# Two transformer blocks on one core: SBUF addresses of the matmul operands moved, so that moving data and weights lie at other distances modulo 256 bytes

## The reference

```python
# first block (modulated by w_ada)
proj = h @ w_in                     # q, k, v, g_ret, u, gate_r, gate_s
y_ret = (silu(g_ret) * ret) @ w_ret_out
glu_a, glu_b = split(y_ssm @ w_s5_glu)
merged = sigmoid(gate_r) * y_ret + sigmoid(gate_s) * (glu_a * sigmoid(glu_b))
x = x + gt_m * rmsnorm(merged @ w_out)
x = x + gt_f * rmsnorm((silu(a) * b) @ w_ffn_out)      # a, b = split(h @ w_ffn_in)
# second block
proj = h @ w_in                     # attention, GLA, convolution and merge columns
mixed = g0 * (o_att @ w_br_attn) + g1 * (o_gla @ w_br_gla) + g2 * (y_conv @ w_br_conv)
x = x + mixed @ w_out
x = x + (silu(h2 @ w_gate) * (h2 @ w_up)) @ w_down
return rms_norm(x)
```

## Time and profile before

| | |
|---|---|
| median of 3 runs | 3368.33 us (3368.28 to 3370.02) |
| the profiled execution, its own time | 3367.02 us |
| its span | 3365.2 us |
| granted TensorE clock, mean over the span | 0.992 |
| PE busy | 3294.1 us (98%) |
| DVE busy | 2325.3 us (69%) |
| ACT busy | 1454.6 us (43%) |

### The profile page before, as it was taken

How to read it: one execution, slowest core, us unless ns; L and a number is a source line. 1 busy time by engine, 2 the same in 40 slices (tenths; PEclk the granted TensorE clock), 3 DMA queues, 4 the chain that set the end, 5 groups by cost and what they waited for, 6 DMA issues and landing times.

```text
span 3365.2 us, 51972 instructions
## 1 busy us (share of the span) xinstructions
PE 3294.1 (98%) x20368; PEld 2916.3 (87%) x20368; DVE 2325.3 (69%) x2503; ACT 1454.6 (43%) x1464; POOL 434.4 (13%) x309
## 2 busy tenths in 40 slices
PE   7999999999999999999899999999999999999998
PEld 3599999999888888888778888888888888888887
DVE  6789979877676666666666567657777766666554
ACT  2256664444444444433454444344344444444332
POOL 1047678500100000000000000000003000000000
PEclk9999999999999999999999999999999999999999
DMA  9884556677545555577534444555555555555554
GB/s 381 347 330 182 181 195 238 242 299 299 225 159 191 189 193 193 184 274 260 214 126 175 163 163 178 196 183 188 193 188 198 188 191 195 187 189 193 187 193 150
DMA packets 119746, 706.34 MB, mean 210 GB/s; under 512 B 13776, under 2 KB 28752, under 8 KB 41312
## 3 DMA queue, kind: packets, MB, share of 16 engines
q1 hardware_dynamic: 109280, 695.96, 56.4%
q10 hardware_dynamic: 10368, 9.02, 0.8%
HBM read 702.83 MB, written 2.10 MB: 209 GB/s over the span
## 4 chain that ended last, share of the span: by engine, by line
PE 86%; DVE 7%; ACT 3%; issue 2%; DMA 1%; SPq 1%; DVEq 0%; ACTq 0%
PE acc L643 44%; PE acc L644 22%; PE acc L640 5%; PE acc L641 5%; PE acc L642 5%; DVE ring_lo L1482 2%; DVE ring_raw L1504 1%; ACT ring_hi L1022 1%; DMA ring_raw<-w_ada 1%; SPq L547 1%; PE p_norm L692 1%; PE p_y L710 1%; PE p_z L720 1%; DVE mg L1497 0%; DVE rstd L1529 0%
## 5 line engine op out<-in xcount | busy, mean ns | idle before, releaser
L1482 DVE TENSOR_TENSOR ring_lo<-ring_raw,ring_hi 128x2048 fp32r<-128x2048 f32 (+2 forms) x560 | 1266.9, 2264 | 560.1 <-ACT ring_hi L1022 559.3
L643 PE MATMUL acc<-h_split,ring_hi 128*128 128x512 f32 x4736 | 1644.0, 392 | 9.7 <-DVE h_split L1544 4.5
L644 PE MATMUL acc<-h_split,ring_lo 128*128 128x256 f32 x4736 | 1318.3, 278 | 0.0
L1022 ACT ACTIVATE ring_hi<-ring_raw 128x2048 fp32r<-128x2048 f32 (+2 forms) x560 | 1042.6, 1866 | 451.0 <-DMA ring_raw<-w_down 148.5
L643 PEld LDWEIGHTS acc<-h_split,ring_hi 128*128 128x128 f32 x4736 | 892.4, 188 | 203.7 <-issue 10.5
L644 PEld LDWEIGHTS acc<-h_split,ring_lo 128*128 128x128 f32 x4736 | 890.6, 188 | 0.4
L643 PE MATMUL acc<-ffn_split,ring_hi 128*128 128x512 f32 x1408 | 483.8, 389 | 0.0
L2151 POOL TENSOR_TENSOR sq_sum<-sq_sum,tile 128x256 f32<-128x256 f32 x60 | 77.0, 1284 | 2548.9 <-ACT tile L1048 2548.9
L644 PE MATMUL acc<-ffn_split,ring_lo 128*128 128x256 f32 x1408 | 390.9, 278 | 0.0
L640 PE MATMUL acc<-h_split,ring_hi 128*128 128x256 f32 x1152 | 330.4, 287 | 0.3 <-ACT val_a L1035 0.2
L641 PE MATMUL acc<-h_split,ring_hi 128*128 128x256 f32 x1152 | 322.3, 280 | 0.0
(11 more groups left out here) (381 smaller groups left out, 3936.4 us busy)
## 6 DMA issues: line engine op xcount, KB each, us to landing
ring_raw<-w_ff SPq DMA_DIRECT2D x88, 1024.0 KB, 4.8
ring_raw<-w_down SPq DMA_DIRECT2D x64, 1024.0 KB, 4.8
ring_raw<-w_ffb SPq DMA_DIRECT2D x56, 1024.0 KB, 4.8
ring_raw<-w_mix SPq DMA_DIRECT2D x48, 1024.0 KB, 4.8
ring_raw<-w_ada SPq DMA_DIRECT2D x32, 1024.0 KB, 11.8
ring_raw<-w_heads SPq DMA_DIRECT2D x32, 1024.0 KB, 4.8
ring_raw<-w_ret SPq DMA_DIRECT2D x32, 1024.0 KB, 4.9
ring_raw<-w_glu SPq DMA_DIRECT2D x32, 1024.0 KB, 4.8
```

What stands on the lines that cost most here:

```text
L643: mm(dst[:], hi[s][:, t, :], moving[:, k, :], start=start, stop=False, skip_group_check=True)
L644: return mm(dst[:, T:], lo[s][:, t, :], moving[:, k, 0:T], start=False, stop=stop, skip_group_check=True)
L1022: run(hi[s][:, 0:n, :], raw[s][:, 0:n, :], COPY).then_inc(hi_done, 1)
L1482: tt(lo[s][:, 0:n, :], raw[s][:, 0:n, :], hi[s][:, 0:n, :], SUB).then_inc(lo_done, 1)
```

## The change

It moves operands in SBUF, by other spacers and by reading two of them at an offset. `normed` and `h_split` get 128 bytes more; the first block's mixer stages use the view 128 bytes further (`normed_mix`, `h_mix`), all later stages the one at the start (`h`). The ring's slots get spacers, so that the slots lie alike modulo 256. No instruction is added or taken away on PE, ACT, POOL or SP, and their order is the same; DVE has two more register instructions.

```diff
-LO_AT = slice(16, 16 + KT * P)
...
-                raw.append(sb(shared, f"ring_raw{s}", [P, KT * P + 32])[:, LO_AT].rearrange("p (k c) -> p k c", k=KT))
-            lo.append(sb(ctx, f"ring_lo{s}", [P, KT * P + 32], F32R)[:, LO_AT].rearrange("p (k c) -> p k c", k=KT))
+                raw.append(sb(shared, f"ring_raw{s}", [P, KT, P]))
+            lo.append(sb(ctx, f"ring_lo{s}", [P, KT, P], F32R))
+            sb(ctx, f"ring_step{s}", [P, 16])
             hi.append(sb(ctx, f"ring_hi{s}", [P, KT, P], F32R))
+            sb(ctx, f"ring_gap{s}", [P, 48])
...
-        sb(ctx, "h_step", [P, 8])
+        sb(ctx, "h_step", [P, 56])
...
-            normed = sb(shared, "normed", [P, KT, 2 * T])
-        h = sb(ctx, "h_split", [P, KT, 2 * T], F32R)
+            normed_words = sb(shared, "normed", [P, KT * 2 * T + 32])
+        h_words = sb(ctx, "h_split", [P, KT * 2 * T + 32], F32R)
+        normed, h, normed_mix, h_mix = (words[:, at:at + KT * 2 * T].rearrange("p (k c) -> p k c", k=KT)
+                                        for at in (0, 32) for words in (normed_words, h_words))
...
-                sb(mixer, "ret_step", [P, 24])
...
-                sb(mixer, "y_step", [P, 24])
+                sb(mixer, "y_step", [P, 8])
...
+                sb(ffn, "f1_step", [P, 32])
...
+                sb(mixer, "o_step", [P, 32])
...
-                y_conv = sb(mixer, "y_conv_split", [P, HALF, 2 * T], F32R)
+                y_conv = sb(mixer, "y_conv_split", [P, HALF * 2 * T + 8], F32R)[:, 4:4 + HALF * 2 * T].rearrange("p (k c) -> p k c", k=HALF)
...
-                    mixed = sb(late, "mixed_split", [P, KT, 2 * T], F32R)
+                    mixed = sb(late, "mixed_split", [P, KT * 2 * T + 8], F32R)[:, 4:4 + KT * 2 * T].rearrange("p (k c) -> p k c", k=KT)
...
+                sb(ffn, "f2_step", [P, 32])
...
-                        ins = products(p, acc[o], o, t, h, t, t == 0, t == KT - 1)
+                        ins = products(p, acc[o], o, t, h_mix if p.thirds else h, t, t == 0, t == KT - 1)
...
-                    product(p, g, o, [(o, 0, 16, h, 0)])
+                    product(p, g, o, [(o, 0, 16, h_mix, 0)])
```

More of the change, by code:

```diff
@@ L738, in heads_values @@
                         for s in range(2):
-                            ins = mm(v_banks[2 * n + s][:], normed[:, k, T + s * P:T + (s + 1) * P], wv[quad % 2][n][:, :, kt, :],
+                            ins = mm(v_banks[2 * n + s][:], normed_mix[:, k, T + s * P:T + (s + 1) * P], wv[quad % 2][n][:, :, kt, :],
                                      start=k == 0, stop=k == KT - 1)
@@ L783, in head_product @@
                 for t in range(KT):
-                    ins = products(p, acc[r // 2][:, half], s, t, h, t, t == 0, t == KT - 1)
+                    ins = products(p, acc[r // 2][:, half], s, t, h_mix, t, t == 0, t == KT - 1)
                 ins.then_inc(slot_free[s], 1)
@@ L818, in _ @@
                         last = (R["done"], HEADS, 2)
-                    product(p, g, m, [(m, 0, 16, ret_flat if m >= 4 else h, 0)], last, ret_bank(p, g, m))
+                    product(p, g, m, [(m, 0, 16, ret_flat if m >= 4 else h_mix, 0)], last, ret_bank(p, g, m))
                     if opening(g) and m == 0:
@@ L829, in _ @@
                     for m in range(4):
-                        product(p, g, m, [(m, 0, 16, h, 0)], None, (m_done, KT - 1 + m) if m < 2 else None)
+                        product(p, g, m, [(m, 0, 16, h_mix, 0)], None, (m_done, KT - 1 + m) if m < 2 else None)
                         if m in S5_TAIL:
@@ L838, in _ @@
                     for i in range(4):
-                        product(p, g, 3 * i, [(2 * i, 0, 16, h, 0)])
+                        product(p, g, 3 * i, [(2 * i, 0, 16, h_mix, 0)])
                         for c in range(2):
@@ L1108, in start @@
                     act.wait_ge(n_done, k + 1)
-                    run(normed[:, k, T:], normed[:, k, T:], ACT.Identity, bias=mod[:, k:k + 1]).then_inc(hf_done, 1)
+                    run(normed_mix[:, k, T:], normed_mix[:, k, T:], ACT.Identity, bias=mod[:, k:k + 1]).then_inc(hf_done, 1)
                     act.wait_ge(hf_done, k + 1)
-                    run(h[:, k, 0:T], normed[:, k, T:], COPY).then_inc(n_hi, 1)
+                    run(h_mix[:, k, 0:T], normed_mix[:, k, T:], COPY).then_inc(n_hi, 1)
                     if k == 3:
@@ L1628, in first_lo @@
                 dve.wait_ge(*((v_step, k + 1) if k < KT - 1 else (v_done, len(v_banks))))
-                tt(h[:, k, T:], normed[:, k, T:], h[:, k, 0:T], SUB).then_inc(h_done, 1)
+                tt(h_mix[:, k, T:], normed_mix[:, k, T:], h_mix[:, k, 0:T], SUB).then_inc(h_done, 1)
             LAG = 2
@@ L1636, in _ @@
                     inverse_std(1)
-                own.step(stt(normed[:, k, T:], x[:, k, :], gain[:, 0, k:k + 1], rstd[:], MUL, MUL))
+                own.step(stt(normed_mix[:, k, T:], x[:, k, :], gain[:, 0, k:k + 1], rstd[:], MUL, MUL))
                 first_row(k, 1, k).then_inc(n_done, 1)
```

## The result

The changed kernel takes 3398.0 us (median of 8 runs, 3379.2 to 3401.8); the kernel before 3368.5 us in the same comparison (8 runs, 3367.4 to 3372.1). The ratio is 1.0073, with a 95% interval of 1.0059 to 1.0086: slower by 30 us, and outside the range of 3337 to 3370. The 8 times fall into two groups, 3379 to 3382 us (3 runs) and 3396 to 3402 us (5 runs), with nothing between. The profiled execution took 3401.06 us, so it is one of the second group; its span is 3399.3 us.

What follows compares the result with a forecast made beforehand. It took TensorE's time per product as the bound. Pair stages 17.7 us plus three-matmul stages 3.8, all else 0, gave 21.5 us off 3368.3; it said 3346 us, range 3337 to 3370.

Steps and rivals of the forecast that it cites:

- What bounds the kernel: Whole kernel: TensorE busy 98% of the span; in ffb PE never idle, DVE 198 us of 307.84, so product time counts.
- a block keeps the pace with which it began: Pair stages: a block's product time, 340, 350 or 353 ns at 192 and 0, holds to its end.
- after the change nothing does: Long stretches: odd blocks reset the pace before; afterwards nothing resets it, so each stretch keeps its first block's pace.
- The rival of no difference: All stages: distances don't matter, as the skill's two read ports would also give; no change, 3368 us, chance 0.06.
- All three even blocks behind such a wait were fast, so I expect fast here: ffa's first block behind the opening pair, after a 0.43 us wait: expected fast, 5.10 us for 15 products.
- the sum's terms of 7.2 and 7.3 us: Gains at 0.11 us per odd block: ffa after opening pair, ffb, down1 (65 blocks); ff2 after first block, down2 (66).
- 13 slow blocks of 20: Even pair blocks behind small matmuls: evidence that ff2 to down2 might be slow; the forecast called fast little above even odds.
- its two rivals: ff2 to down2 slow at 350 ns, 3367 us, chance 0.25; with ffa to down1 slow too, 3388 us, 0.12.
- both settle at 350 ns: ffa to down1 and ff2 to down2 both slow: 3388 us, chance 0.12, decided by ffa's first block behind the opening pair.
- The second stretch: Last iteration of conv, mrg0 and slot 1 of mix: 30 odd blocks faster, 3.3 us gained.
- The new distances: ret, merged, y_ssm, mixed, y_conv at distances no row showed: taken as 0, ends 7.3 us either way, more likely 3.
- Mix slow after y_conv: Mix: y_conv leaves a slow pace for h; 56 blocks cost 6 us instead of gaining 2, 3354 us, chance 0.13.

Runs made afterwards that it cites:

- the repeat: The changed kernel run once more, unchanged, to profile another execution; 3375.23 us, one run.
- the known distances: Changed kernel with ret, merged, y_ssm, y_conv and mixed moved to meet the weights at 64 and 128; 3389.77 us.
- the 64 bytes: Changed kernel with the ring, h and everything behind 64 bytes further, distances between moving operand and weights kept; 3407.63 us.
- the control: Changed kernel plus 4 throw-away products at each of two places, ahead of ffa's first block behind the opening pair and ff2's second, reading h at 192 and 0; 3400.57 us.
- the two runs with slot 3 moved: Changed kernel with slot 3 back at 64 and 128: 3369.57 us; the same plus ret, merged, y_ssm, y_conv, mixed moved to known distances: 3351.99 us.
- the run with eight products: Changed kernel plus 8 throw-away products at 64 and 128 ahead of ffa's first block behind the opening pair and ff2's second; 3364.23 us.

## Why the prediction was wrong

**What bounds the kernel** was read rightly. ffb stayed PE's alone, with DVE at 198 us of 313.6 and no wait, and the sum over products explains all but 3.2 of the 34.1 us of difference, where the prediction had asked for 2.

**That distances set the pace** was right, and so was "a block keeps the pace with which it began": no stretch of ffa to down1 or of ff2's second block to down2, in any profile at 192 and 0 throughout, changed its pace; PE had no wait in them. But "after the change nothing does", of what resets the pace, left out the waits: in the first profile the one of 0.45 us ahead of conv's ninth block turned 340 into 350 ns, to the end of mrg0, and in the repeat the one in mrg0 did. The rival of no difference does not hold: products of the same shapes took 340, 347, 350 and 353 ns with the clock at 1.00. The Trainium skill (TensorE: Matmul & The Clock Gate, step-by-step in Part 2) gives the streamed operand and the weight load a read port each; these times contradict what the prediction drew from that, equal time for equal instructions, and no run here tells what in the reads makes the difference.

**The step that failed** is the sentence "All three even blocks behind such a wait were fast, so I expect fast here", and with it the sum's terms of 7.2 and 7.3 us. In ten profiled long stretches that were entered at 192 and 0 with nothing ahead to reset them (two each of the changed kernel, its repeat, the known distances, the 64 bytes and the control) three ran at 340, six at 350 and one at 353 (the first stretch 2 of 5 at 340, the third 1 of 5); the entry differs between executions of one program. The four entries of the two runs with slot 3 moved were at 350 as well, until slot 3 came. The prediction gave the first stretch far better than even odds from three cases of a single execution, and for the third it counted 13 slow blocks of 20 and still gave slow only 0.37 in its two rivals. The three cases were also unlike what was to come: before the change the product ahead of each of these waits was at 64 and 128 (slot 1 of the opening pair, slot 3 in conv, slot 1 in mrg0), after it none is. Even such a product is no warrant: in the two runs with slot 3 moved, conv's eighth block ran at 347 ns in slot 3, its ninth began 0.16 and 0.18 us late, and ran at 353 and 350 ns. So three fast of three was in part luck. The first stretch then cost 14.8 us more (the rival had 13.7), the third 13.3 (13.8). This is the rival "both settle at 350 ns", with a chance of 0.12 and a time of 3388 us, and the place that was to decide it, ffa's first block, decided it. Three of the eight executions, those at 3379 to 3382 us, had by their times only one of the two slow.

**Between the rival's 3388 and 3398 us** lie the smaller terms. The second stretch gained nothing: conv and mrg0 lost 2.8 us in place of gaining, mix won 0.4. The new distances were taken as 0, with 7.3 us as the end. Against 64 and 128 they cost some 10 us; against before, where these operands met the slots at two pairs of distances in turn, the products of these operands took 4.4 us more: 1.1 in out1, 1.6 in out2, 0.8 by y_conv (45.2 us in place of 44.5), 0.9 by ret and y_ssm. The three-matmul products with h took 408.5 us in place of 412.4, 3.8 us less as forecast. Less the 0.9, the stages u to glu won 2.9 us in their products, but PE waited 2.0 us more for `o_t`, so less than half of it arrived in this execution.

**Mix slow after y_conv**, chance 0.13, did not come in the changed kernel, where h ran at 340 ns behind every y_conv (208 and 16) of the profile. At the same addresses, in the run with eight products, it was at 350 once behind a y_conv. It came with slot 3 moved, y_conv at 80 and 144, where mix took 314.3 us against 307.4 before, 6.9 us for the 6 that were worked out.

**What the change was worth** had both entries been fast can be read from the profile of the run with eight products, whose long stretches are fast. Its products take 3026.0 us without the added ones, 13.7 us less than before, where the forecast was 21.5: the two long stretches give 13.9 of 14.5, the second 0.2 of 3.3, the stages u to glu 2.0 of 3.8, and out1 and out2 lose 2.6 where they were put at 0. That execution was the fastest of its ten. From their median, 3364 us, less 5.9 us of added products, the changed kernel with fast entries would take some 3358 us and not 3346; this is an estimate.

## What to carry to other kernels

Where the moving operand and the weights of the same matmul are read from SBUF, don't lay all buffers alike because one of two distances looks faster. The fast blocks may owe their pace to the slow ones between them. Look at each stretch's first block, in several executions, and at what follows each wait. Keep something in or ahead of the stretch that sets the pace (here one slot of four at 64 and 128, or six throw-away products there, 2 us a stretch). Two groups of times, tens of microseconds apart with nothing between, can be the sign of such a pace. Here the gap of 20 us was 130 blocks at 5.60 us in place of 5.44.

## What the runs showed of the hardware

- The same pair of matmuls on the same addresses has several steady paces: 340, 350 and 353 ns at distances 192 and 0, 347 and 353 ns at 64 and 128. 96 and 160 gave 357 ns a three-matmul product, 176 and 240 gave 353 a pair. A pace lasted up to 131 blocks, 733 us at 5.60 us each, without a change.
- A wait of PE of 0.2 us can change the pace: at 192 and 0 on both sides, 340 became 350 or 353 ns in mrg0 in four profiles.
- At 64 and 128 an entry through 357, 343 and 352 or 353 ns settles at 347 within six products; 340 follows if the next block is at 192 and 0. Cut short at four, 350 followed (twice); where the entry was at 346 or 347 from the second product on, four were enough (three times).
- Why an entry falls one way or the other, and differs between executions of one program, stays open: no run varied the moment of entry by itself. What in SBUF or TensorE makes the paces was not shown either.
